# Two-layer mLSTM and attention encoder on one core: a projection block ahead of the second transposes, the last head's queues reordered, two MLP units issued seven eighths at a time

## What is computed

```python
h = concat([meta, x])                      # 528 x 1024, float32
for i in range(2):
    y = rmsnorm(h, g[i, 0])
    y = mlstm_mixer(y) if i == 0 else diff_attention(y)    # 8 heads each
    h = h + y
    h = h + square(relu(rmsnorm(h, g[i, 1]) @ w_up[i])) @ w_down[i]   # 4096 wide
return rmsnorm(h, final_gain)[16:]

# diff_attention, per head: two score matrices of width 64, block-causal mask
p = softmax(mask(q1 @ k1.T)), softmax(mask(q2 @ k2.T))
o = (p[0] - lam * p[1]) @ v                # v is 128 wide
o = o * rsqrt(mean(o * o) + eps) * gain    # then all heads @ w_out
```

## Time and profile before

| | |
|---|---|
| median of three runs | 1241.19 us |
| the profiled execution | 1241.61 us |
| its span | 1239.9 us |
| TensorE busy | 1207.3 us (97%) |
| VectorE, ScalarE busy | 855.8 us (69%), 659.8 us (53%) |
| POOL busy | 66.0 us (5%) |
| chain that ended last | PE 72%, issue 19%, DVE 5%, ACT 3% |

### The profile page before, as it was taken

How to read it: one execution, slowest core, us unless ns; L and a number is a source line. 1 busy time by engine, 2 the same in 40 slices (tenths; PEclk the granted TensorE clock), 3 DMA queues, 4 the chain that set the end, 5 groups by cost and what they waited for, 6 DMA issues and landing times.

```text
span 1239.9 us, 21705 instructions
## 1 busy us (share of the span) xinstructions
PE 1207.3 (97%) x8549; PEld 1129.0 (91%) x8549; DVE 855.8 (69%) x1340; ACT 659.8 (53%) x1112; POOL 66.0 (5%) x105
## 2 busy tenths in 40 slices
PE   7999999999999999999999999998999999999997
PEld 6999999999999999999989988886787998988986
DVE  5778778666668377487468888785675874855852
ACT  4676776633526246246357777775443452543542
POOL 4121120000000000001010000000000000000000
PEclk9999999999999999999999999999999999999999
DMA  6434323232332323333132122212323232232321
GB/s 166 106 81 108 85 76 103 73 103 69 103 98 99 111 69 103 103 96 110 52 85 69 52 68 68 85 35 68 108 96 102 69 124 87 96 130 75 103 69 68
DMA packets 141600, 110.63 MB, mean 89 GB/s; under 512 B 22104, under 2 KB 139920, under 8 KB 141520
## 3 DMA queue, kind: packets, MB, share of 16 engines
q1 hardware_dynamic: 140000, 104.93, 27.9%
q0 software_dynamic: 1392, 4.49, 1.4%
q10 hardware_dynamic: 128, 0.09, 0.0%
HBM read 107.38 MB, written 2.13 MB: 88 GB/s over the span
## 4 chain that ended last, share of the span: by engine, by line
PE 72%; issue 19%; DVE 5%; ACT 3%; POOL 1%; DMA 0%; DVEq 0%; POOLq 0%; ACTq 0%
PE ps L1927 33%; PE ps L1963 19%; PE ps L1705 15%; PE ps L1755 1%; PE ps L1773 1%; DVE tf L1455 1%; PE ps L1864 1%; ACT wh L628 1%; DVE tbuf L1416 0%; DVE wl L1093 0%; ACT ah L873 0%; PE ps L1840 0%; DVE tl L1468 0%; DVE lo L1314 0%; DMA meta_in<-in_meta_tokens_dram 0%
## 5 line engine op out<-in xcount | busy, mean ns | idle before, releaser
L1927 PE MATMUL ps<-ah,hi 128*128 128x264 f32 (+1 forms) x768 | 206.3, 323 | 3.9 <-DVE al L1406 3.9
L1927 PE MATMUL ps<-al,hi 128*128 128x264 f32 (+1 forms) x768 | 206.0, 323 | 0.0
L1927 PE MATMUL ps<-ah,lo 128*128 128x264 f32 (+1 forms) x768 | 205.3, 321 | 0.0
L628 ACT ACTIVATE hi<-raw 128x1024 fp32r<-128x1024 f32 (+1 forms) x128 | 121.6, 970 | 135.1 <-PE ps L1927 135.1
L1705 PE MATMUL ps<-yh,wh 128*128 128x264 f32 (+1 forms) x704 | 160.6, 302 | 0.0
L1705 PE MATMUL ps<-yl,wh 128*128 128x264 f32 (+1 forms) x704 | 155.6, 295 | 0.0
L1705 PE MATMUL ps<-yh,wl 128*128 128x264 f32 (+1 forms) x704 | 155.4, 295 | 0.0
L1927 PEld LDWEIGHTS ps<-ah,hi 128*128 128x128 f32 x768 | 127.7, 189 | 15.9 <-DVE al L1406 4.5
L1927 PEld LDWEIGHTS ps<-al,hi 128*128 128x128 f32 x768 | 127.9, 189 | 11.2
L1927 PEld LDWEIGHTS ps<-ah,lo 128*128 128x128 f32 x768 | 127.8, 189 | 11.2
L1420 DVE TENSOR_TENSOR h<-ps,h 128x528 f32<-128x528 f32 (+1 forms) x64 | 44.7, 698 | 110.9 <-PE ps L1927 110.9
(11 more groups left out here) (271 smaller groups left out, 2615.0 us busy)
## 6 DMA issues: line engine op xcount, KB each, us to landing
raw<-in_mlp_w_up_dram SPq DMA_DIRECT2D x32, 1024.0 KB, 5.4
raw<-in_mlp_w_down_dram SPq DMA_DIRECT2D x32, 1024.0 KB, 5.1
raw<-in_diff_w_in_dram SPq DMA_DIRECT2D x24, 512.0 KB, 3.7
raw<-in_mlstm_w_in_dram SPq DMA_DIRECT2D x16, 512.0 KB, 4.3
raw<-in_mlstm_w_in_dram SPq DMA_DIRECT2D x16, 256.0 KB, 5.4
raw<-in_mlstm_w_out_dram SPq DMA_DIRECT2D x3, 1024.0 KB, 5.1
raw<-in_diff_w_out_dram SPq DMA_DIRECT2D x3, 1024.0 KB, 5.1
mbc<-gate_rows POOLq DMA_DIRECT2D x8, 264.0 KB, 5.8
```

The costliest lines, as they stand in the source:

```text
L628: return nc.scalar.activation(o, i, ACT.Copy, scale=scale)
L1927: last = mm(ps[:, b + s, 0:cw], x[half][:, 20 * m + kb, :], y[:, kb, c0:c0 + cw], start=(kb == 0 and n == 0), stop=(kb == CB - 1 and n == 2))
```

## The change

1. **Steady attention heads.** Where there is a next head, block kb 2 of its key unit is issued between `scores` of tile 2 and `turn` of tile 1, instead of behind that `turn`.
2. **Last head of mLSTM.** ScalarE's weight splits of output units 2 and 3 move behind the squares of the denominator and behind the Ln; VectorE's second low part moves behind the product that follows the Ln.
3. **Last attention head.** `turn` of tile 3 comes two blocks earlier and is followed by `turn_meta` in bank 5, which no longer waits for bank 6; the output blocks around are dealt out anew. In all heads ScalarE makes the square and its high part ahead of `zf`. For the last head VectorE makes `sql1` in place of POOL. The z parts of head 6 are made in step 8, behind the meta copies.
4. **MLP.** At i = 4, 12, 20, 28 both units are issued up to their seventh block, then the last block of (i, 0), then that of (i, 1). The waits of each unit stand at its first block.

```diff
@@ scalar, step0
-                elif exists(hd):
-                    act.wait_ge(unit_done, U_OUT0)
-                    split(U_OUT0 + 2, 2, 0)
-                    split(U_OUT0 + 3, 3, 0)
...
                     nc.scalar.activation(acc[:, QSPLIT:T], ps[:, B_ND + 1, 0:T - QSPLIT], ACT.Square).then_inc(den_sq, 1)
+                    if not nxt:
+                        act.wait_ge(unit_done, U_OUT0)
+                        split(U_OUT0 + 2, 2, 0)
...
                     nc.scalar.activation(acc[:, :], acc[:, :], ACT.Ln).then_inc(hln_done, 1)
+                    if not nxt:
+                        split(U_OUT0 + 3, 3, 0)
@@ scalar, step1
+            def z_hi(hd):
+                act.wait_ge(z_mul1, hd + 1)
+                copy(ah[:, ds(hd, 1), NMETA:T].rearrange("p o t -> p (o t)"), zf[:, :]).then_inc(zh_rd1, 1)
...
-                    copy(att_meta[0:16, :], ps[0:NMETA, B_TR1, :]).then_inc(meta_rd, 1)
+                    b = B_TR1 if exists(hd) else B_SC[1] + 1
+                    copy(att_meta[0:16, :], ps[0:NMETA, b, :]).then_inc(meta_rd, 1)
                     act.wait_ge(meta_rd, hd)
                     copy(att_meta[64:80, :], att_meta[0:16, :].bitcast(F32)).then_inc(meta_dup, 1)
+                    if not exists(hd):
+                        z_hi(hd - 2)
...
+                    nc.scalar.activation(abuf[:, NMETA:T], ps[:, B_PV1, :], ACT.Square).then_inc(pv_sq1, 1)
+                    act.wait_ge(pv_sq1, hd)
+                    copy(sqh1[:, :], abuf[:, NMETA:T]).then_inc(sq_hi1, 1)
                     wait(act, z_ready, hd + (HEADS - 1))
-                    copy(zf[:, :], ps[:, B_PV1, :], gains[:, ds(hd + 39, 1)])
-                    nc.scalar.activation(abuf[:, NMETA:T], ps[:, B_PV1, :], ACT.Square).then_inc(pv_rd1, 1)
-                    act.wait_ge(pv_rd1, hd)
-                    copy(sqh1[:, :], abuf[:, NMETA:T]).then_inc(sq_hi1, 1)
+                    copy(zf[:, :], ps[:, B_PV1, :], gains[:, ds(hd + 39, 1)]).then_inc(pv_rd1, 1)
@@ vector, step0: split(U_OUT0 + 3, 3) moves behind the product that gives e_done
@@ vector, step1
+                elif exists(hd - 1):
+                    meta_lo(hd - 1, B_SC[1] + 1)
+                    z_lo(hd - 2)
...
+                if isinstance(hd, int) and hd == HEADS:
+                    dve.wait_ge(sq_hi1, HEADS)
+                    V.tensor_tensor(sql1[:, :], abuf[:, NMETA:T], sqh1[:, :].bitcast(F32), ALU.subtract).then_inc(sq_lo1, 1)
@@ tensor, mlp
-                def plain(i, m):
+                def plain(i, m, first, end):
+                    if first == 0:
+                        plain_waits(i, m)
...
                 for i, item in pe_order():
+                    if not is_up(i) and i % 8 == 4 and item in (0, 1):
+                        if item == 0:
+                            plain(i, 0, 0, CB - 1)
+                            plain(i, 1, 0, CB - 1)
+                        plain(i, item, CB - 1, CB)
+                    elif item in (0, 1):
+                        plain(i, item, 0, CB)
@@ tensor, turn_meta
+                if b == B_TR1:
+                    pe.wait_ge(vtl_rd1, min(n + 2, HEADS) if isinstance(n, int) else n + 2)
+                    pe.wait_ge(atl_rd, n * 4 + 4)
+                else:
+                    pe.wait_ge(exp_done[1], 4 * HEADS)
@@ tensor, step1
                 if not exists(hd) and exists(hd - 1):
-                    out_part(2, 0, 6)
+                    out_part(2, 0, 4)
                 if exists(hd - 1):
                     turn(hd * 4 - 1, 3)
+                if not exists(hd) and exists(hd - 1):
+                    turn_meta(hd - 1, B_SC[1] + 1)
+                    out_part(2, 4, 6)
+                    out_part(3, 0, 1)
...
                 if exists(hd - 1):
                     output(hd - 1, 1 - par)
+                if not exists(hd) and exists(hd - 1):
+                    out_part(3, 1, 4)
...
                     scores(hd * 4 + 2, 2, par)
+                if exists(hd) and nxt:
+                    part(n1, 1, 2, 3)
+                if exists(hd):
                     turn(hd * 4 + 1, 1)
-                if nxt:
+                if exists(hd) and nxt:
+                    part(n1, 1, 3, CB)
+                elif nxt:
                     part(n1, 1, 2, CB)
...
                 if exists(hd - 1):
                     squares(hd - 1)
+                if not exists(hd) and exists(hd - 1):
+                    out_part(3, 4, 6)
+                    out_part(0, 6, 7)
+                    out_part(1, 6, 7)
@@ after the loop
-            for k in range(4):
+            for k in range(2, 4):
                 out_part(k, 6, 7)
             for k in range(4):
                 out_part(k, 7, CB)
```

More of the change, by code:

```diff
@@ L617, in _ @@
             nc.gpsimd.memset(att_meta[:, :].bitcast(F32), 0.0).then_inc(mask_made, 1)
-            with pool.Fori(0, HEADS) as i:
+            with pool.Fori(0, HEADS - 1) as i:
                 pool.wait_ge(sq_hi1, i + 1)
@@ L1066, in step1 @@
                     split_unit(n1 * 3 + (U_IN1 + 4), 1, 1, n1 + 1)
-                if exists(hd - 1):
-                    act.wait_ge(z_mul1, hd)
-                    copy(ah[:, ds(hd - 1, 1), NMETA:T].rearrange("p o t -> p (o t)"), zf[:, :]).then_inc(zh_rd1, 1)
+                if exists(hd - 1) and not (isinstance(hd, int) and hd == HEADS - 1):
+                    z_hi(hd - 1)
             heads_loop(act, 1, step1)
@@ L1277, in step0 @@
                     V.scalar_tensor_tensor(acc[:, :], acc[:, :], -0.5, of[par][:, :], ALU.mult, ALU.add).then_inc(e_done, 1)
+                    if not nxt:
+                        split(U_OUT0 + 3, 3)
                 if nxt and not first:
@@ L1604, in values_lo, with meta_lo, z_lo @@
                                 vmeta[par][0:16, :].bitcast(F32), ALU.subtract).then_inc(vtl_rd1, 1)
-            def meta_lo(hd):
+            def meta_lo(hd, b=B_TR1):
                 dve.wait_ge(meta_rd, hd + 1)
-                V.tensor_tensor(att_meta[32:48, :], ps[0:NMETA, B_TR1, :],
+                V.tensor_tensor(att_meta[32:48, :], ps[0:NMETA, b, :],
                                 att_meta[0:16, :].bitcast(F32), ALU.subtract).then_inc(metal_rd, 1)
+            def z_lo(hd):
+                dve.wait_ge(zh_rd1, hd + 1)
+                V.tensor_tensor(blk(al, hd)[:, NMETA:T], zf[:, :], blk(ah, hd)[:, NMETA:T].bitcast(F32),
+                                ALU.subtract).then_inc(z_ready, 1)
             def step1(hd, par, pair):
@@ L1672, in step1 @@
                     split(n1 * 3 + (U_IN1 + 4), 1)
[L1673 to L1677, removed]
+                if exists(hd - 1) and not (isinstance(hd, int) and hd == HEADS - 1):
+                    z_lo(hd - 1)
             heads_loop(dve, 1, step1)
@@ L1900, in mlp, with plain_waits @@
                 u_out = (U_OUT0, U_OUT1)[layer]
-                def plain(i, m):
+                def plain(i, m, first, end):
+                    if first == 0:
+                        plain_waits(i, m)
+                    b, half = plain_bank(layer, i, m), 1 - i % 2
+                    mh, ml = (yh, yl) if is_up(i) else (ah, al)
+                    for kb in range(first, end):
+                        if (i, m) == (0, 0):
+                            pe.wait_ge(y_ready, 8 * norm + kb + 1)
+                        if not is_up(i) and i % 8 == 4 and m == 0:
+                            pe.wait_ge(a_ready, 8 * (4 * layer + i // 8) + kb + 1)
+                        for n, (x, y) in enumerate(((hi, mh), (hi, ml), (lo, mh))):
+                            for s, (c0, cw) in enumerate(spans):
+                                last = mm(ps[:, b + s, 0:cw], x[half][:, 20 * m + kb, :], y[:, kb, c0:c0 + cw],
+                                          start=(kb == 0 and n == 0), stop=(kb == CB - 1 and n == 2))
+                    if end == CB:
+                        last.then_inc(m_done, 1)
+                def plain_waits(i, m):
                     pe.wait_ge(m_lo, ready + READY[i, m])
@@ L1917, in plain @@
                         pe.wait_ge(c_done, 7 * ranks + summed(PAIRS - 5, (("U3", "U4"), ("C12", "C21"))[i - PAIRS + 4][m]))
-                    b, half = plain_bank(layer, i, m), 1 - i % 2
-                    mh, ml = (yh, yl) if is_up(i) else (ah, al)
-                    for kb in range(CB):
-                        if (i, m) == (0, 0):
-                            pe.wait_ge(y_ready, 8 * norm + kb + 1)
-                        if not is_up(i) and i % 8 == 4 and m == 0:
-                            pe.wait_ge(a_ready, 8 * (4 * layer + i // 8) + kb + 1)
-                        for n, (x, y) in enumerate(((hi, mh), (hi, ml), (lo, mh))):
-                            for s, (c0, cw) in enumerate(spans):
-                                last = mm(ps[:, b + s, 0:cw], x[half][:, 20 * m + kb, :], y[:, kb, c0:c0 + cw],
-                                          start=(kb == 0 and n == 0), stop=(kb == CB - 1 and n == 2))
-                    last.then_inc(m_done, 1)
```

(4 more changed lines are left out.)

17 lines of the change are left out of this document (5 added, 12 removed).

## The result

| | before | after |
|---|---|---|
| median on the same chip | 1241.23 us (1241.01 to 1242.5) | 1231.9 us (1230.96 to 1233.24) |
| ratio | | 0.9924, 95% interval 0.9914 to 0.9934 |
| the profiled execution | 1241.61 us | 1232.41 us |
| its span | 1239.9 us | 1230.7 us |

A forecast was written before the change was run, and what follows sets the result against it. TensorE, busy 97% of the span, was taken as the bound, so only closed gaps counted. Terms 3.1 + 1.7 + 3.9 + 1.3 = 10.0 took 1241.61 to 1231.6, less 0.42 for the median: 1231.2 us, range 1228.4 to 1235.6.

The forecast's parts named there:

- Part 1: Steady attention heads: a block ahead of the second transposes closes a 0.51 us wait in six heads; 3.1 us (2.0 to 3.2).
- The rival that the loop becomes bound by other engines: Attention loop becomes bound by VectorE and ScalarE, so the block ahead of the transposes gives nothing: 1234.3; 5%.
- Part 2: Last mLSTM head: TensorE's wait for the squares goes, z still last by 0.3; 1.7 us (0.9 to 1.9).
- Part 3: Last attention head: output and squares come earlier, so unit 4 starts at 853.6 instead of 857.5; 3.9 us (3.0 to 4.2).
- the third wait: Last attention head: TensorE's wait of 0.76 at 854.08 goes, since squares and six blocks last past z.
- the fourth of 0.42: End of attention heads: unit 4's wait for a weight split, 0.42 at 857.50, stays; only four blocks lie beside it.
- Part 4: MLP: the first groups win 1.0 and 2.4, six later groups lose 0.35 each; 1.3 us (-0.2 to 3.4).
- I count the 1.5 with the gap: Second MLP, first group: the 1.5 us lost at 1.2 GHz behind the 2.18 gap counts as gained with it.
- the eight evacuations that I had named: MLP: TensorE waits for an evacuation in all eight groups, 0.25 plus 0.1 of restart, 0.35 a group.
- both rivals at 10%: Low-clock stretch of layer 1 stays, 1232.7; or evacuation waits don't bite in the six later groups, 1229.1; 10% each.
- the one that halves part 3: Last attention head: reordered queues fail, squares or meta_lo wait longer, that term halved: 1233.2; 8%.
- The slower one: MLP: eight new short gaps each drop the clock, costing 12.3 us against the 10.0 gained: 1243.5; 2%.

The follow-up runs named there:

- the other profile of before: The kernel before, unchanged, profiled once more for its clock; 1239.7 us in one execution.
- part 4 alone: Only the new order of the first MLP down units, against the kernel before; 1240.96 us, ratio 0.9996 (0.9986 to 1.0006).
- part 2 alone: Only the moved weight splits in the last mLSTM head, against the kernel before; 1239.03 us, ratio 0.9979 (0.997 to 0.9989).

## Why the prediction held, step by step

The forecast was 1231.2 and the range 1228.4 to 1235.6; the kernel takes 1231.9. The sum of the terms, 10.0, is also what the ledger shows when the start is left out (9.2 + 0.8). That it agrees to the tenth is luck in two ways. Parts 1 and 2 gave 0.6 more than their terms, part 4 0.5 less and part 3 0.1 less. And 1.5 of the sum is there only because the one profile of before that the forecast rests on has a low-clock stretch at 934: against the other profile of before the ledger sums to 8.5. (The terms' ends, 5.7 and 12.7, taken from 1241.2, give 1228.5 to 1235.5; the range on record is 0.1 wider on either side.)

- **Part 1 (3.1, measured 3.6).** The mechanism was right, and VectorE and ScalarE had the slack that the earlier trace rows show. Mis-sized: a head gave 0.575 and not 0.51, the difference being about the restart of 0.07 behind the wait, and the first head, at nothing, gave 0.1. The rival that the loop becomes bound by other engines is wrong.
- **Part 2 (1.7, measured 1.85).** Right, with z late by 0.3.
- **Part 3 (3.9, measured 3.8).** `output` came at 836.94, 2.95 earlier against the head's start where 3.2 was worked out; the squares start at 841.38, 0.19 after TensorE could have gone on (0.2 worked out, and no bracket shows it), the third wait is gone and the fourth of 0.42 has stayed. One sentence failed, "Reordering zf behind the squares in the other heads leaves the sum on ScalarE unchanged": true of the sum, but the order alone is worth 1.2 us in the kernel before. It had no effect on the forecast only because part 1 closes the same wait.
- **Part 4 (1.3, by the profiled executions 0.8, by the medians of that part alone about 0).** Here a step failed: "So I count the 1.5 with the gap." The argument was that two shorter gaps had no low clock behind them, and it took one profile for the rule. (A rival at 10% let the stretch stay in the changed kernel; that the kernel before could itself be without it had no place in the sum.) The gap has the low clock in some executions of the same kernel and not in others. Without it the gain of the second MLP's first group is 2.27 - 1.53 = 0.74, and part 4 loses: 0.86 + 0.74 - 2.41 = -0.8. With it: +0.7. The ratio of part 4 alone, 0.9996, lies between. The rest of this term was right in kind: the eight evacuations that I had named do bite, and cost 0.40 each in the later groups (forecast 0.35). The wait of (4, 1) in layer 1 was put at 0.4, which is its bracket; by starts it costs 0.6. In the first groups (5, 0) waits as well as (5, 1), where I had let one take the place of the other; the total still came within 0.15.
- **The rivals.** No low-clock stretch lies in the second MLP in the profile of the changed kernel, and the waits on the evacuations bite in all six later groups, so both rivals at 10% didn't happen, nor did the one that halves part 3. The slower one is wrong too: ten waits of some 0.2 to 0.5 us at bank turns, and the clock is 1.00 behind each. The rule of the Trainium skill ("TensorE: Matmul & The Clock Gate", section "A second HAM failure mode: psum-queue depth-cycling") that I had set beside it isn't borne out by waits of this length: the 12.3 us worked out beside it weren't lost, nor any part of them.

That the median came out 0.7 above the forecast has no single cause that I could show. The two things that scatter between executions, the wait at 23.8 and the low stretches, are each larger than that.

## What to carry to other kernels

When a new order lets a matmul group start earlier, read the semaphore **count** of the wait at its head: a count that was one evacuation too strict had cost nothing before and cost 2.9 us afterwards. Price each short wait of TensorE by the distance of starts and not by the idle column, which here shows 0.16 of 0.39 lost. And before a term rests on a low-clock stretch, look whether another execution of the same kernel has it.

## What the runs showed of the hardware

- A gap of 2.2 us in TensorE's work was followed by a stretch of 3.4 us at 1.2 GHz in four profiles of seven, and by none in three, one of them of the same kernel. None of the six profiles without the gap has one there. The stretch costs 1.5 us. The gap of 1.7 in the first MLP had none in any of the seven profiles that have it; at the start of the mLSTM heads, behind a wait of 1.5 for the values' first head at 43, nine profiles of thirteen have one. The length of a gap alone doesn't tell.
- A stretch at 1.2 GHz costs nothing where TensorE has to wait soon after anyway. From the first value transpose of mLSTM head 0, at 43, to that of head 1 it is 25.7 to 26.2 us in eight profiles with a stretch of 3.4 us and in four with none: the wait for VectorE's `plo` in between is 1.3 to 1.6 without it and at most 0.8 with it. Only in the profile of part 2 alone, whose stretch lasts 6.8, is it 27.0.
- A wait of TensorE costs 0.23 us beyond what the idle column shows when it is for an evacuation (0.16 of modelled end, 0.07 of a slower first matmul or pair), alike for pairs of 264 columns and for 512, and 0.26 when it is for `al` or `wl`. The Trainium skill, "Perfetto Trace Analysis", section "Tensor Engine Instruction (MATMUL, LD_WEIGHTS)", says that a matmul's end is estimated by the profiler and not observed, which goes with this.
- Executions of one kernel differ by up to 3.8 us here (1239.29 to 1243.13 in 22 of the kernel before on one chip). Differences of 0.2 to 0.6 us can be read only from landmarks within traces.
